# Causal convolution of 31 taps: 18 taps on VectorE and 13 on TensorE instead of 16 and 15, with three small steps of the same layer put elsewhere

## The reference, cut to what matters

```python
def even_mixer(h, w_in, sc_conv_w, cf_conv_w, cf_conv_b, cf_ln_g, cf_ln_b, w_out):
    z = h @ w_in
    sc_b, sc_c, sc_x, cf_a, cf_g = jnp.split(
        z, [SC_WIDTH, 2 * SC_WIDTH, 3 * SC_WIDTH, 3 * SC_WIDTH + CF_WIDTH], axis=-1)
    y_sc = sc_b * causal_dwconv(sc_c * sc_x, sc_conv_w)      # 3 taps
    u = cf_a * jax.nn.sigmoid(cf_g)
    u = causal_dwconv(u, cf_conv_w) + cf_conv_b              # 31 taps
    u = jax.nn.silu(layernorm(u, cf_ln_g, cf_ln_b))
    return jnp.concatenate([y_sc, u], axis=-1) @ w_out
```

## Time and profile before

| | us |
|---|---|
| three runs | 1613.48, 1613.65, 1613.69 (median 1613.65) |
| span of the profiled execution, first to last instruction | 1611.7 |
| what the median has beyond that span | 1.95 |
| PE busy | 1589.0 (99%) |
| DVE busy | 1262.0 (78%) |
| ACT busy | 855.1 (53%) |

### The profile page before, as it was taken

The page is one execution under the profiler, slowest core; times in us unless marked ns, Lnnn a source line. Parts: engine busy times, 40 slices in busy tenths (PEclk is TensorE's granted clock), DMA queues, the critical chain, the costliest instruction groups (busy, mean ns, idle before and its releaser), DMA issues.

```text
span 1611.7 us, 26970 instructions
## 1 busy us (share of the span) xinstructions
PE 1589.0 (99%) x11042; PEld 1451.2 (90%) x11044; DVE 1262.0 (78%) x1447; ACT 855.1 (53%) x1025; POOL 58.6 (4%) x76
## 2 busy tenths in 40 slices
PE   9999999999999999999999999999999999999998
PEld 8989999988898999899998899999899998899997
DVE  7978889877678997878878697885878887785555
ACT  6566555555465545644446474445544455564443
POOL 3001000000010000000000010000000000010000
PEclk9999999999999999999999999999999999999999
DMA  9414988644238885498864349875598854265552
GB/s 266 162 53 161 349 300 304 217 158 147 79 119 299 299 290 180 146 325 310 314 216 135 112 158 329 314 243 183 173 324 301 308 167 160 93 196 183 185 194 76
DMA packets 231438, 343.48 MB, mean 213 GB/s; under 512 B 7066, under 2 KB 194048, under 8 KB 231360
## 3 DMA queue, kind: packets, MB, share of 16 engines
q1 hardware_dynamic: 230304, 340.94, 62.4%
q0 software_dynamic: 752, 1.18, 0.2%
q10 hardware_dynamic: 304, 0.27, 0.1%
HBM read 341.32 MB, written 1.05 MB: 212 GB/s over the span
## 4 chain that ended last, share of the span: by engine, by line
PE 80%; DVE 10%; issue 6%; ACT 3%; DMA 0%; DVEq 0%; ACTq 0%
PE PS L666 21%; PE PS L768 19%; PE PS L667 11%; PE PS L657 9%; PE PS L635 5%; PE PS L738 3%; DVE wl L1507 3%; PE PS L644 3%; PE PS L694 2%; PE PS L905 2%; ACT wh L1078 1%; DVE XL L1523 1%; DVE Z L1606 1%; PE PS L832 1%; PE PS L854 1%
## 5 line engine op out<-in xcount | busy, mean ns | idle before, releaser
L1507 DVE TENSOR_TENSOR wl<-raw,wh 128x2048 fp32r<-128x2048 f32 (+2 forms) x256 | 570.1, 2229 | 147.3 <-ACT wh L1078 145.3
L666 PE MATMUL PS<-HP,wh 128*128 128x512 f32 x1728 | 608.0, 395 | 2.1 <-DVE wl L1507 2.1
L1078 ACT ACTIVATE wh<-raw 128x2048 fp32r<-128x2048 f32 (+2 forms) x256 | 475.5, 1859 | 134.0 <-PE PS L768 114.9
L667 PE MATMUL PS<-HP,wl 128*128 128x256 f32 x1728 | 484.6, 280 | 0.0
L666 PEld LDWEIGHTS PS<-HP,wh 128*128 128x128 f32 x1728 | 324.0, 188 | 76.7 <-DVE wl L1507 2.5
L768 PE MATMUL PS<-FX,wh 128*128 128x256 f32 x1920 | 345.0, 281 | 0.4 <-DVE FX L1672 0.4
L667 PEld LDWEIGHTS PS<-HP,wl 128*128 128x128 f32 x1728 | 326.5, 189 | 0.0
L768 PEld LDWEIGHTS PS<-FX,wh 128*128 128x128 f32 x1920 | 294.5, 188 | 2.9 <-issue 0.6
L768 PE MATMUL PS<-FX,wl 128*128 128x256 f32 x960 | 269.9, 281 | 0.0
L768 PEld LDWEIGHTS PS<-FX,wl 128*128 128x128 f32 x960 | 180.4, 188 | 0.0
L1606 DVE SCALAR_TENSOR_TENSOR Z<-ada,CA,Z 128x1024 f32 x126 | 161.4, 1281 | 1.3
(11 more groups left out here) (286 smaller groups left out, 1752.7 us busy)
## 6 DMA issues: line engine op xcount, KB each, us to landing
ada<-ada_w SPq DMA_DIRECT2D x144, 512.0 KB, 6.0
raw<-ffn_w_gate SPq DMA_DIRECT2D x66, 1024.0 KB, 5.4
raw<-ffn_w_up SPq DMA_DIRECT2D x66, 1024.0 KB, 5.4
raw<-ffn_w_down SPq DMA_DIRECT2D x66, 1024.0 KB, 5.0
raw<-od_w_in SPq DMA_DIRECT2D x13, 1024.0 KB, 5.3
raw<-ev_w_in SPq DMA_DIRECT2D x10, 1024.0 KB, 8.1
raw<-w_in SPq DMA_DIRECT2D x8, 1024.0 KB, 5.4
raw<-w_out SPq DMA_DIRECT2D x8, 1024.0 KB, 5.8
```

The costliest lines, as they stand in the source:

```text
L666: mm(pairs(bank(bk)), lhsT=lhs(0, k), rhs=HP[:, k], start=k == 0, stop=False, skip_group_check=True)
L667: last = mm(bank(bk, 0, S), lhsT=lhs(1, k), rhs=HH[:, k, :], start=False, stop=k == k_tiles - 1, skip_group_check=True)
L1078: last = A_(dst(wh), src, ACT.Copy)
L1507: last = tt(dst(wl), src, dst(wh).bitcast(F32), ALU.subtract)
```

## The change

The number of DVE's taps goes from 16 to 18, so that TensorE and ACT have 52 taps and diagonals for the four tiles and not 60. The first tap of the short convolution goes from DVE to ACT, behind ACT's diagonals. The product sc_c * sc_x goes up in DVE's order, to behind tap k = 14. `lru_cols` goes down in DVE's order, from behind k = 6 to between the subtraction of the mean and the reciprocal of the root. The loop for the low parts of units stands as it did.

```diff
-DVE_TAPS = 16
+DVE_TAPS = 18
 ...
+            act.wait_ge(z_out, 9)
+            for t in range(4):
+                A_(cols(Z, EV["C"], 4)[:, t, :], cols(Z, EV["P"], 4, 2 + S)[:, t, 0:S], ACT.Copy,
+                   scale=pc("scw", t)).then_inc(ev("sc_first"), 1)
 ...
-                if k == 6:
-                    lru_cols()
                 if k % 2 == 1 and due:
                     lo(due.pop(0))
-
-            dve.wait_ge(w_used, n0 + 10)
-            own.wait(padded)
-            SP_ = cols(Z, EV["P"], 4, 2 + S)
-            for i in range(2):
-                tt(SP_[:, 2 * i:2 * i + 2, 2:], pairs(bank(2 + i)), pairs(Z[:, EV["C"] + 512 * i:][:, 0:512]),
-                   ALU.mult).then_inc(z_out, 1)
-            dve.wait_ge(z_out, 9)
+                if k == DVE_TAPS - 4:
+                    dve.wait_ge(w_used, n0 + 10)
+                    own.wait(padded)
+                    SP_ = cols(Z, EV["P"], 4, 2 + S)
+                    for i in range(2):
+                        tt(SP_[:, 2 * i:2 * i + 2, 2:], pairs(bank(2 + i)), pairs(Z[:, EV["C"] + 512 * i:][:, 0:512]),
+                           ALU.mult).then_inc(z_out, 1)
+
             C = cols(Z, EV["C"], 4)
             marks = []
-            for k in range(3):
+            for k in (1, 2):
                 for t in range(4):
                     w = pc("scw", 4 * k + t)
-                    if k == 0:
-                        marks.append(own.mark(ts(C[:, t, :], SP_[:, t, 0:S], w, None, ALU.mult)))
+                    if k == 1:
+                        dve.wait_ge(ev("sc_first"), t + 1)
                     else:
-                        own.wait(marks[4 * (k - 1) + t])
-                        marks.append(own.mark(stt(C[:, t, :], SP_[:, t, k:k + S], w, C[:, t, :], ALU.mult, ALU.add)))
+                        own.wait(marks[t])
+                    marks.append(own.mark(stt(C[:, t, :], SP_[:, t, k:k + S], w, C[:, t, :], ALU.mult, ALU.add)))
 ...
             stt(Dv, over(bank(7, 0, S), 4), -1.0 / CF, V, ALU.mult, ALU.add).then_inc(ev("ln_diff"), 1)
 
+            lru_cols()
             dve.wait_ge(ev("ln_diff"), 1)
```

## The result

The changed kernel takes 1617.55 us (median of 16 runs, 1616.88 to 1619.08), the kernel before 1613.67 (16 runs, 1613.27 to 1615.54). The ratio is 1.0023, 95% interval 1.0016 to 1.0030: 3.9 us slower. 1617.3 was forecast, by case A.

The account below looks back on a forecast made before the run. TensorE, busy 99%, bounds the kernel before; after the change DVE's taps do. The sums' +1.70 and the constants' +0.06 give 1.76, with 1.9 for the clock 3.65 later: 1617.3 us, range 1615.0 to 1619.2.

Parts of the forecast that it names:

- case A: TensorE's clock falls during its new idle time: +3.0 to +6.1, centre +3.65, 1617.3 us; chance 0.58.
- The moved constants free nothing, the stall takes all: DVE before the low part of n0+11: without `lru_cols` (4.09) the stall grows from 2.59 to 6.68, gain nil.
- VectorE 1.99 later, the sums for the mean 1.70: DVE adds the first half of V at 100.01, +1.99; TensorE's four sums end at about 102.75, +1.70.
- ScalarE's four taps hidden, 1.8 long, 2.8 to spare: ACT's first short-convolution taps, behind its diagonals: done by 92.7, before DVE wants them at 95.51.
- TensorE idle about 5.0: TensorE stands from its last tap at 95.69 until DVE has added the first half of V at 100.7.
- The constants in the wait for the root, +0.06: `lru_cols` in DVE's idle 3.95 before the reciprocal: 5.24 instead of 5.18, bounds 0 to 0.3.
- The clock falls, +1.9: After TensorE's idle time its matmuls cost twice: four sums 1.5 later, +1.9 taken between +1.7 and +4.3.
- the forecast's lower bound: Low clock level lasting 3.6 us after TensorE restarts, some +1.7 in all.
- Two times, by the rule of the Trainium skill: Whole kernel: either +1.8 or some 2 more, the median of a few runs near the commoner time.
- B: DVE late but clock kept: +1.76, 1615.4 us, range 1615.0 to 1616.3; chance 0.34.

Follow-up runs that it names:

- e_lru6: The changed kernel with the recurrence constants (`lru_cols`) back behind tap 6: 1617.29 us, ratio to the kernel before 1.0021.
- e_late16_before: The kernel before, with the low parts of n0+11 and n0+12 moved behind taps 13 and 15: 1613.42 us, ratio 1.0000.
- e_spin22: The changed kernel with 22 products with zeroes on TensorE between its last tap and the first sum for the mean: 1615.55 us, ratio to before 1.0010.
- e_taps16: The changed kernel with 16 taps on VectorE instead of 18, leaving only the three moves: 1613.83 us, ratio to before 1.0001.
- e_spin8: The changed kernel with 8 products with zeroes on TensorE behind its last tap, leaving 3.33 us idle: 1616.98 us, ratio to before 1.0020.

## Why the prediction was right, point by point

- *The moved constants free nothing, the stall takes all.* Right: 6.68 forecast and measured, and e_lru6 shows it. It holds only as long as the stall stands (see e_late16_before).
- *VectorE 1.99 later, the sums for the mean 1.70.* Right within 0.1: counted from the start of the taps, the first half of V is added 2.00 later (26.79 against 24.79) and the sums start 1.62 later; with the clock held the runs are 1.78 slower in all against 1.76 forecast (e_spin22).
- *ScalarE's four taps hidden, 1.8 long, 2.8 to spare.* Right: 1.71 and 2.9. With fewer taps on VectorE (e_taps16) they are not hidden, as more diagonals stand ahead of them; there nothing hung on it.
- *TensorE idle about 5.0.* Right: 5.07.
- *The constants in the wait for the root, +0.06.* Not visible in the kernel after: the root came later, because of the clock, and VectorE waited 0.54 for it. In e_taps16, at full pace, VectorE goes from the constants to the reciprocal without a wait, and the reciprocal starts 107.47 - 74.38 = 33.09 behind the start of the taps, against 33.04: +0.05.
- *The clock falls, +1.9.* The mechanism was right, the size a little low: +2.54 in one profile, +2.13 in the other (e_lru6), 2.0 by medians (1617.55 - 1615.55). The four sums lost 1.87 and not 1.5. Their seven gaps lost 1.46, as forecast (the eight starts spread over 3.15 us and not 1.69); the forecast left out that the last matmul is itself longer, 0.63 and not 0.38, and that the first starts anew. The half unit lost 0.69 in the kernel after and 0.28 in e_lru6, where 1.9 - 1.5 leaves 0.4. What it loses goes by how long the low level lasts into the work: 5.2 us in the kernel after (102.17 to 107.4), 4.3 in e_lru6, 3.6 in the forecast's lower bound. So it differs from one execution to the next, and profile and median need not agree. That the choice near the lower bound came out so well is in part luck: its reason, that the work at the kernel's start was full of gaps, was not tested, and the profile after shows that start in another form (last section).
- *Two times, by the rule of the Trainium skill* ("TensorE: Matmul & The Clock Gate", section "Part 1: The HAM clock gate"). The rule that the gate watches on its own schedule agrees with the moments of the falls: 3.4 us after the last tap in the kernel after and 2.5 in e_lru6, with the same gap, and in e_spin8 only after work had begun again. That the kernel would therefore take one of two times isn't borne out for an idle time of 5.07: none of 16 runs lies below 1616.88, where 1615.4 would be the time with the clock kept. The chance of B, 0.34, looks too high.

## What to carry to other kernels

Before work is taken off an engine, look for its next stall: where that stall ends at a moment set by another engine, all that is saved ahead of it is lost, and what is added behind it counts, as soon as the engine has no time left to give. Fill such a stall with work of the engine that waits for nobody, and only then shift the balance. Here the new order alone brought nothing, the change alone cost 3.9 us, and both together brought 3.5. And where TensorE comes to stand for some us, reckon the slow restart as well, or compare with a run in which products with zeroes fill the gap.

## What the runs showed of the hardware

- The granted clock fell after idle times of TensorE of 5.07, 5.06 and 3.33 us, and at the kernel's start after 2.58 and 2.23. It stayed after 1.75, 1.83 and 2.04. It can fall when TensorE has already begun again (1.3 us after, in e_spin8).
- The falls at the kernel's start are in two of the twelve profiles, in a stage that the change doesn't touch. In the profiled execution after, TensorE in order of time:

```profile
5.64 1.09 PE L870 MATMUL PS<-CN,Z 128*128 128x128 f32 x8
6.95 1.09 PE L870 MATMUL PS<-CN,Z 128*128 128x128 f32 x8 [0.21 <-DMA Z<-x]
7.88 3.19 PE L674 MATMUL PS<-ZB 128*128 128x512 bf16 x14
13.64 0.39 PE L635 MATMUL PS<-FX,wh 128*128 128x256 f32 x1 [2.58 <-DVE wl L1781]
```

  The same place in the kernel before (its 14 products with zeroes are in the earlier trace rows):

```profile
5.65 3.67 PE L870 MATMUL PS<-CN,Z 128*128 128x128 f32 x16 [0.23 <-DMA Z<-x]
13.77 0.39 PE L635 MATMUL PS<-FX,wh 128*128 128x256 f32 x1 [0.97 <-DVE wl L1777]
```

  The first product with weights starts no later than before. But the transposes of x ahead of it (L870) are at full pace, eight in 1.09 us, where 16 took 3.67. So the low level of the start had already ended before 5.64, and the 14 products with zeroes were through at 11.07 and not at 12.79. TensorE then stood for 2.58 us and not 0.97; the clock fell at about 15.2, 1.6 into its next work, and stayed low past 18:

```profile
14.00:16.00 2.00, 2.00 (x17) 2.00 (x16) 2.00 (x4) 2.00 (x4) 1.33 (x2) 0.80 1.11 354
16.00:18.00 2.00, 2.00 (x11) 2.00 (x11) 2.00 (x3) 1.65 (x2) 2.00 (x4) 0.50 1.07 373
```

  In the profiled execution of e_taps16 the same place has a wait of 2.23, and the clock fell there too:

```profile
13.47 0.39 PE L635 MATMUL PS<-FX,wh 128*128 128x256 f32 x1 [2.23 <-DVE wl L1781]
```

```profile
14.00:16.00 2.00, 2.00 (x15) 2.00 (x15) 2.00 (x4) 2.00 (x3) 1.50 (x2) 0.73 1.12 357
```

  The slow start accounts for the 1.41 us by which all starts later in the profile after: the first 32 products with weights (L635) take 5.59 us and not 4.06, and start 0.13 earlier, which gives 1.40. The other changed kernels, whose first 40 us are the same, start their taps at 73.26 to 73.52. Why the low level of the start ends earlier in some executions is open. The prediction's reading that 3.60 us of dense work at the start don't bring the pace back holds for the execution that it read and not for this one.
